# Turning queries and keys on VectorE in 32x32 blocks: a two-layer attention trunk in split fp32

## What is computed

```python
hdn = rms_norm(x, norm_g[i])
q, k, v, z = jnp.split(hdn @ w_in, 4, axis=-1)
q = apply_rope(rms_norm(split_heads(q, N_HEADS), q_norm), cos, sin)   # layer 1: no rope
k = apply_rope(rms_norm(split_heads(k, N_HEADS), k_norm), cos, sin)
s = jnp.einsum('bhqd,bhkd->bhqk', q, k) * d ** -0.5                   # layer 1: + c_q - c_k
y = jnp.einsum('bhqk,bhkd->bhqd', jax.nn.softmax(causal(s)), v)
x = x + (merge_heads(y) * jax.nn.silu(z)) @ w_out[i]
```

## Time and profile before

| | |
|---|---|
| time of three runs, us | 565.17, 565.41, 566.66 |
| the profiled execution's own time, us | 564.39 |
| its span (first to last instruction), us | 562.6 |
| granted TensorE clock over the span | 1.0 |
| busy share: PE, DVE, ACT, POOL | 99%, 60%, 45%, 53% |
| bytes read from HBM, written | 47.48 MB, 2.11 MB |

### The profile page before, as it was taken

One profiled execution on the slowest core, in us unless ns is written; L12 is line 12 of the kernel. 1 busy time (PEld: TensorE's weight loads), 2 busy tenths in 40 slices (PEclk: granted clock), 3 DMA queues, 4 the chain that ended last, 5 costly groups with the idle time before them and its releaser, 6 DMA issues.

```text
span 562.6 us, 9761 instructions
## 1 busy us (share of the span) xinstructions
PE 554.5 (99%) x3086; PEld 512.2 (91%) x3086; DVE 336.4 (60%) x863; ACT 250.4 (45%) x761; POOL 299.5 (53%) x348
## 2 busy tenths in 40 slices
PE   6999999999999999999999999999999999999998
PEld 4999999999999999888898999999999999998887
DVE  3687676767575758472563284746574747564621
ACT  5746262626262626251545454545454545443300
POOL 4766363636362627253655594746574748471700
DMA  9814131313131322122423362615150616040221
GB/s 258 237 38 135 57 93 58 95 56 93 56 93 56 93 56 93 56 77 94 121 58 80 91 138 31 135 35 137 33 152 17 143 28 161 19 149 4 75 94 56
DMA packets 78237, 49.94 MB, mean 89 GB/s; under 512 B 4090, under 2 KB 71418, under 8 KB 78211
## 3 DMA queue, kind: packets, MB, share of 16 engines
q1 hardware_dynamic: 78208, 49.61, 32.8%
q10 hardware_dynamic: 2, 0.00, 0.0%
HBM read 47.48 MB, written 2.11 MB: 88 GB/s over the span
## 4 chain that ended last, share of the span: by engine, by line
PE 96%; DMA 1%; ACT 1%; issue 1%; POOL 1%; DVE 1%; SPq 0%; DVEq 0%; POOLq 0%
PE banks L341 26%; PE banks L342 26%; PE banks L343 26%; PE banks L466 5%; PE banks L451 3%; PE banks L424 2%; PE banks L440 2%; PE banks L439 2%; PE banks L438 2%; PE banks L373 1%; DMA first_raw<-in_a_w_in_dram 1%; ACT probs L648 0%; PE banks L492 0%; PE banks L493 0%; POOL sin_t L1123 0%
## 5 line engine op out<-in xcount | busy, mean ns | idle before, releaser
L1046 POOL TENSOR_TENSOR w_lo<-w_raw,w_hi 128x512 fp32r<-128x512 f32 x147 | 188.1, 1307 | 59.8 <-ACT w_hi L596 59.8
L341 PE MATMUL banks<-w_hi,hT_hi 128*128 128x384 f32 x512 | 175.8, 343 | 2.1 <-DVE hT_lo L785 2.1
L342 PE MATMUL banks<-w_lo,hT_hi 128*128 128x384 f32 x512 | 171.9, 336 | 0.0
L343 PE MATMUL banks<-w_hi,hT_lo 128*128 128x384 f32 x512 | 171.8, 335 | 0.0
L341 PEld LDWEIGHTS banks<-w_hi,hT_hi 128*128 128x128 f32 x512 | 96.6, 189 | 2.7 <-POOL w_lo L1046 2.4
L1062 POOL TENSOR_TENSOR msq<-ssq,eps 128x2 f32<-128x2 f32 x64 | 15.6, 243 | 153.3 <-ACT junk L632 153.2
L342 PEld LDWEIGHTS banks<-w_lo,hT_hi 128*128 128x128 f32 x512 | 96.7, 189 | 0.0
L343 PEld LDWEIGHTS banks<-w_hi,hT_lo 128*128 128x128 f32 x512 | 96.5, 189 | 0.0
L596 ACT ACTIVATE w_hi<-w_raw 128x512 fp32r<-128x512 f32 x148 | 85.0, 643 | 24.5 <-DMA w_raw<-in_b_w_in_dram 19.1
L632 ACT ACTIVATE junk<-banks 128x128 bf16<-128x128 f32 x128 | 34.0, 271 | 110.1 <-PE banks L343 110.0
L908 DVE RECIPROCAL gz<-gz 128x128 f32<-128x128 f32 x64 | 58.2, 933 | 0.5
(11 more groups left out here) (109 smaller groups left out, 891.3 us busy)
## 6 DMA issues: line engine op xcount, KB each, us to landing
w_raw<-in_b_w_in_dram SPq DMA_DIRECT2D x64, 256.0 KB, 4.3
w_raw<-in_a_w_in_dram SPq DMA_DIRECT2D x52, 256.0 KB, 2.9
w_raw<-in_w_out_dram SPq DMA_DIRECT2D x32, 256.0 KB, 3.0
first_raw<-in_a_w_in_dram SPq DMA_DIRECT2D x12, 256.0 KB, 5.6
cos_t<-c_rows SPq DMA_DIRECT2D x8, 256.0 KB, 3.7
out_dram<-xs SPq DMA_DIRECT2D x7, 256.0 KB, 2.1
xs<-in_x_dram SPq DMA_DIRECT2D x3, 512.0 KB, 5.7
xs<-in_x_dram SPq DMA_DIRECT2D x2, 256.0 KB, 2.9
```

The source lines that it names most:

```text
L341: pe.matmul(dst, ah, bh, start=first and m == 0, stop=False)
L342: pe.matmul(dst, ah, bl, start=False, stop=False)
L343: mm = pe.matmul(dst, al, bh, start=False, stop=last and m == n - 1)
L1046: pool.tensor_tensor(w_lo[:, slot, k, :], raw, f32(w_hi[:, slot, k, :]), ALU.subtract).then_inc(wlo_set, by)
```

## The change

TensorE no longer turns queries and keys. VectorE does, in blocks of 32x32: for the two token tiles of one portion, 16 instructions, each of which takes 32 partitions (32 tokens) and, of both q and k and of two tiles, 32 channels, and writes to 32 other partitions of banks 6 and 7. A head has two portions (tiles 0 and 1, tiles 2 and 3), so 32 such instructions. In each engine's period the order is new. The bank of `values` moves from 7 to 3. The plus one of the gate and the division of the probabilities go from DVE to ACT. In `first` the call of TensorE is gone and DVE makes both portions at the end. The core of the diff (the definitions of `silu` and `normalise` move to ACT with the same calls otherwise):

```diff
-        Z_BANK, QT_BANK, Y_BANK = 2, 6, 7
+        Z_BANK, Y_BANK, QT_BANK = 2, 3, 6
 # TensorE
-            def turn_qk(layer, h):
-                pe.wait_ge(qkn_set, TILES * (g + 1))
-                wait(pe, qkTlo_set, 2 * g)
-                wait(pe, y_gated, g)
-                for m in range(2):
-                    for t in range(TILES):
-                        mm = pe.transpose(banks[:, QT_BANK + m, t * P:(t + 1) * P], qkn[:, t, m, :], ident[:, :])
-                    mm.then_inc(qk_turned, 1)
             def scores(layer, h, s):
                 pe.wait_ge(qkTlo_set, 2 * (g + 1))
                 wait(pe, pTlo_set, 3 * g)
+                wait(pe, y_gated, g)
             def period(layer, h, s):
                 qkv(layer, h + 1, 1 - s, 0)
+                qkv(layer, h + 1, 1 - s, 1)
                 scores(layer, h, s)
-                qkv(layer, h + 1, 1 - s, 1)
                 qkv(layer, h + 1, 1 - s, 2)
+                qkv(layer, h + 1, 1 - s, 3)
                 turn_probs(layer, h)
-                qkv(layer, h + 1, 1 - s, 3)
+                zproj(layer, h + 1, 1 - s)
                 values(layer, h, s)
-                zproj(layer, h + 1, 1 - s)
-                turn_qk(layer, h + 1)
             def last(layer):
-                pe.wait_ge(ylo_set, g - 1)
-                pe.wait_ge(vlo_set, TILES * g)
-                project(layer, 0, 0, range(7), True, False)
-                scores(layer, h, 1)
-                project(layer, 0, 1, range(7), True, False)
+                pe.wait_ge(ylo_set, g - 2)
+                pe.wait_ge(qkn_set, TILES * g)
+                project(layer, 0, 0, range(6), True, False)
+                project(layer, 0, 1, range(2), True, False)
+                scores(layer, h, 1)
+                project(layer, 0, 1, range(2, 6), False, False)
+                pe.wait_ge(ylo_set, g - 1)
+                project(layer, 0, 0, [6], False, False)
+                project(layer, 0, 1, [6], False, False)
 # ACT
+            def normalise(layer, h):
+                for n, t in enumerate(T_ORDER):
+                    p = probs[:, P_COL[t]:P_COL[t] + P * (t + 1)]
+                    act.wait_ge(rinv_set, TILES * g + n + 1)
+                    act.activation(p, p, ACT.Copy, scale=rinv[:, t:t + 1]).then_inc(probs_set, 1)
             def exp_z(layer, h):
+                act.wait_ge(ez_set, g + 1)
+                act.activation(gz[:, 0, :], gz[:, 0, :], ACT.Copy, bias=1.0).then_inc(ez1_set, 1)
+            def begin(layer, h):
+                split_qk(layer, h)
+                if not isinstance(h, int) or h > 0:
+                    split_y(layer, h - 1)
             def period(layer, h, s):
+                begin(layer, h)
                 read_qkv(layer, h + 1, 1 - s, 0)
-                split_w(layer, h + 2, s, (0, 1, 2, 3))
+                split_w(layer, h + 2, s, (0, 1, 2))
+                read_qkv(layer, h + 1, 1 - s, 1)
                 exps(layer, h)
-                read_qkv(layer, h + 1, 1 - s, 1)
+                split_w(layer, h + 2, s, (3,))
+                normalise(layer, h)
                 split_w(layer, h + 2, s, (4,))
                 read_qkv(layer, h + 1, 1 - s, 2)
+                split_w(layer, h + 2, s, (5,))
+                read_qkv(layer, h + 1, 1 - s, 3)
                 split_probs(layer, h)
-                split_w(layer, h + 2, s, (5, 6, 7))
-                read_qkv(layer, h + 1, 1 - s, 3)
-                split_y(layer, h)
-                split_qk(layer, h + 1)
+                split_w(layer, h + 2, s, (6, 7))
                 exp_z(layer, h + 1)
 # DVE
+            def turn_qk(layer, h, ts):
+                dve.wait_ge(qkn_set, TILES * g + ts.stop)
+                for a in range(QUADS):
+                    tokens = qkn[a * QUAD:(a + 1) * QUAD, ts, :, :].rearrange("p t m c -> p m t c")
+                    for b in range(QUADS):
+                        turned = banks[b * QUAD:(b + 1) * QUAD, QT_BANK:QT_BANK + 2, ts.start * P:ts.stop * P].rearrange("p m (t c) -> p m t c", c=P)
+                        at = dve.transpose(turned[:, :, :, a * QUAD:(a + 1) * QUAD], tokens[:, :, :, b * QUAD:(b + 1) * QUAD])
+                at.then_inc(qk_turned, 1)
+            def begin(layer, h):
+                late = not isinstance(h, int) or h > 0
+                if late:
+                    gate_y(layer, h - 1)
+                split_qk(layer, h)
+                if late:
+                    low_y(layer, h - 1)
             def period(layer, h, s):
-                silu(layer, h)
+                begin(layer, h)
                 silu_part(layer, h, 0)
+                silu_part(layer, h, 1)
                 split_v(layer, h + 1, 1 - s, 0)
                 norm_qk(layer, h + 1, 0)
+                silu_part(layer, h, 2)
                 maxima(layer, h)
-                silu_part(layer, h, 1)
-                normalise(layer, h)
                 split_v(layer, h + 1, 1 - s, 1)
                 norm_qk(layer, h + 1, 1)
-                silu_part(layer, h, 2)
+                invert_sums(layer, h)
                 silu_part(layer, h, 3)
-                split_probs(layer, h)
+                turn_qk(layer, h + 1, slice(0, 2))
                 split_v(layer, h + 1, 1 - s, 2)
                 norm_qk(layer, h + 1, 2)
                 split_v(layer, h + 1, 1 - s, 3)
-                gate_y(layer, h)
                 norm_qk(layer, h + 1, 3)
-                low_y(layer, h)
-                split_qk(layer, h + 1)
+                split_probs(layer, h)
+                turn_qk(layer, h + 1, slice(2, 4))
 # POOL, period
-                split_w(layer, h + 2, s, (0, 1, 2, 3))
+                split_w(layer, h + 2, s, (0, 1, 2))
                 rstd_qk(layer, h + 1, 1)
-                split_w(layer, h + 2, s, (4,))
+                split_w(layer, h + 2, s, (3, 4))
                 rstd_qk(layer, h + 1, 2)
-                split_w(layer, h + 2, s, (5, 6, 7))
+                split_w(layer, h + 2, s, (5,))
                 rstd_qk(layer, h + 1, 3)
+                split_w(layer, h + 2, s, (6, 7))
```

More of the change, by code:

```diff
@@ L47 @@
 DVE_FIRST = (3, 5, 7)
+QUAD = 32
+QUADS = P // QUAD
 def build_trunk(nc, x, norm_g, w_out, a_w_in, a_q_norm, a_k_norm, b_w_in, b_f_bias, b_q_norm,
@@ L458, in values @@
                 pe.wait_ge(vlo_set, TILES * (g + 1))
-                wait(pe, qkTlo_set, 2 * (g + 1))
                 parts = ((v_hi, pT_hi), (v_hi, pT_lo), (v_lo, pT_hi))
@@ L832, in norm_qk @@
                                   rot[:, t % 2, :, :], ALU.add).then_inc(qkn_set, 1)
+            def turn_qk(layer, h, ts):
+                g = HEADS * layer + h
+                dve.wait_ge(qkn_set, TILES * g + ts.stop)
[5 more added lines that the diff above has]
+                at.then_inc(qk_turned, 1)
             def split_qk(layer, h):
@@ L859, in maxima, with invert_sums @@
                                              accum_out=negmax[:, t:t + 1]).then_inc(max_set, 1)
-            def normalise(layer, h):
+            def invert_sums(layer, h):
                 g = HEADS * layer + h
@@ L894, in low_y @@
                                   ALU.subtract).then_inc(ylo_set, 1)
-            def silu(layer, h):
-                g = HEADS * layer + h
-                dve.wait_ge(ez_set, g + 1)
-                dve.tensor_scalar(gz[:, 0, :], gz[:, 0, :], 1.0, None, ALU.add).then_inc(ez1_set, 1)
             def silu_part(layer, h, n):
@@ L988, in first @@
                     norm_qk(layer, 0, 3)
-                split_qk(layer, 0)
+                for half in range(2):
+                    turn_qk(layer, 0, slice(2 * half, 2 * half + 2))
+            def begin(layer, h):
[5 more added lines that the diff above has]
+                    low_y(layer, h - 1)
             def period(layer, h, s):
-                silu(layer, h)
+                begin(layer, h)
                 silu_part(layer, h, 0)
+                silu_part(layer, h, 1)
                 split_v(layer, h + 1, 1 - s, 0)
                 norm_qk(layer, h + 1, 0)
+                silu_part(layer, h, 2)
                 maxima(layer, h)
-                silu_part(layer, h, 1)
-                normalise(layer, h)
                 split_v(layer, h + 1, 1 - s, 1)
                 norm_qk(layer, h + 1, 1)
-                silu_part(layer, h, 2)
+                invert_sums(layer, h)
                 silu_part(layer, h, 3)
-                split_probs(layer, h)
+                turn_qk(layer, h + 1, slice(0, 2))
                 split_v(layer, h + 1, 1 - s, 2)
@@ L1006, in period @@
                 split_v(layer, h + 1, 1 - s, 3)
-                gate_y(layer, h)
                 norm_qk(layer, h + 1, 3)
-                low_y(layer, h)
-                split_qk(layer, h + 1)
+                split_probs(layer, h)
+                turn_qk(layer, h + 1, slice(2, 4))
             def last(layer):
                 h = HEADS - 1
-                silu(layer, h)
+                begin(layer, h)
+                silu_part(layer, h, 0)
```

(6 more changed lines are left out.)

10 lines of the change are left out of this document (2 added, 8 removed).

## The result

The changed kernel takes 570.39 us (median of five runs, 568.78 to 572.97); the kernel before took 565.17 in five runs beside it. The ratio is 1.0106 (95% interval 1.0087 to 1.0124): slower by 1.1% (by the two medians alone, 0.9%), where 1.1% faster was forecast. The profiled execution is the slowest of the five, 572.97 us with a span of 571.2, so the terms read from it add up to 8.6 us of span and not to the medians' 5.2. Part of that is the clock: TensorE's mean granted clock is 0.988 in this execution and 0.991 in each of the other four.

A forecast was written before the change was run, and what follows sets the result against it. TensorE's list of work was taken to bound the kernel. -14.1 + 6.8 + 0.8 + 1.4 - 0.9 = -6.0 us on the profiled 564.39 gave 558.4, the median 1.0 above: 559.4 us; range 552.0 to 574.0.

The forecast's parts named there:

- What bounds the kernel: Periods of both layers: as long as TensorE's list of work, 27.9 to 28.0 us, so only what leaves it can gain.
- TensorE's gain: Turns of queries and keys leave TensorE: 16 pieces of 0.88 us, 14.1 us in all, periods of 27.05 us.
- The block instruction: VectorE's turn: 0.30 us each, a little over 0.286, run to its end; 32 a head make 9.6 us.
- 0.8 us in all: Layer 0's last six periods and `last`: 0.1 us of waiting in each, as VectorE's list of 26.9 nears TensorE's 27.05.
- the text's own slope: Whole kernel: each 0.01 us of block instruction above 0.30 costs 2.7 us.
- Rival C: Layer 0: VectorE becomes the bound, values wait for `pT_lo` every period; slower above 0.322 us, 574.1 at 0.354; chance 0.28.
- The start of layer 0: First head: TensorE waits 3.7 us for scores, 1.7 for bank 0, 0.2 at tile 3, 1.2 at values; 6.8 together.
- The start of layer 1: First head: TensorE waits 0.8 us for the scores, then 0.6 for bank 0; 1.4 together.
- The walk of the queues: Start of layer 1: queries and keys turned at 320.6, split at 322.6, TensorE there at 321.8.
- What was said to go: Start of layer 1: TensorE's 0.9 us wait for the divisions goes, since probabilities are turned a tile later.
- ACT's and POOL's new work and order: Periods: ACT gains 2.6 us on 13.0, POOL makes its last two `w_lo` later; both counted at nothing.
- the sign: Whole kernel: faster, by 6.0 us; chance 0.64 of faster by over 0.3%, 0.27 of slower.

The follow-up runs named there:

- run 4: Changed kernel with the turn's two loops exchanged, so four block instructions in a row write one partition group and read four; 569.31 us in one run.
- run 5: Changed kernel with each block instruction cut in two, one for queries and one for keys (64 of 32x64 a head); 587.49 us in one run.
- run 12: Changed kernel where, in each layer's first period, ACT reads tile 0 ahead of its copies of the turned queries and keys; 567.59 us in one run.
- run 1: Changed kernel with all turns of queries and keys given back to TensorE, the new order kept; 563.59 us, ratio 0.9986 to the kernel before.
- run 3: Changed kernel with the first head of each layer turned by TensorE, the other seven by VectorE; 557.64 us, ratio 0.9884 to the kernel before.
- run 9: Changed kernel with one 32x256 portion, first heads on TensorE, and the gate's second and third reciprocals behind the inverted sums; 554.80 us, ratio 0.9826.
- run 7: Changed kernel with one 32x256 portion, first heads on TensorE, and the next head's tile 0 normed ahead of the gate's first two reciprocals; 563.35 us, ratio 0.9988.

## Why the prediction was wrong

**What bounds the kernel, and TensorE's gain: right.** The periods of layer 1 went from 27.96 to 27.08 us, 0.88 less. Sixteen times 0.88 is the 14.1 us.

**The block instruction: the term that was mis-sized.** The step reads "I take 0.30 us"; it is 0.335, between the ends that the rows gave. The reason given for it was right, an instruction that changes partition groups is run to its end (runs 4 and 5), but the allowance "a little over" 0.286 was too small: the instruction itself takes 0.322 and the next starts 0.013 later. Why it takes 0.322 and not 0.286, whether for the bank that it writes or for the reordering, no run separates. With it VectorE's list in layer 0 is 17.3 + 10.7 = 28.0 us and the periods are 28.04, about 1 us over TensorE's list in each of seven, where 0.8 us in all was allowed. By the text's own slope, 3.5 hundredths x 2.7 = 9.5 us, the forecast of 559.4 becomes 568.9. That this is near the 570.39 is partly luck: the slope has layer 0 some 3 us too high (8.6 for 6.7 in its periods, 8.5 for 7.2 in its start) and makes up with it for most of what is missing at the start of layer 1. Rival C is what happened, at the place it named (`pT_lo` in each period of layer 0 and nowhere in layer 1) and beyond its turning point of 0.322. The Trainium skill's 311 ns for 128x128 bf16 ("VectorE: DVE Perf Modes", "The three transpose paths") is nearer to the 322 ns of this trace than my choice was, and would still have promised a gain. Its rule on held instructions, in the section "Two Vector instructions with no wait between them" of the same page, agrees with the traces of runs 4 and 5, for the inputs' groups too.

**The start of layer 0: near, and in part by luck.** 6.8 us were forecast at 0.30 us, which at 0.335 would be 8.5. Measured: scores at 52.13, 13.05 us behind the gate projection (8.4 of them two tiles: 4.7 waited), and a first period of 30.6 us, 2.5 over the later ones: 7.2. The split of it was other than told: TensorE ran at the lower clock where it was to wait for bank 0. That cost nothing more, as VectorE has no idle time from 50.8 to 72.2 us and TensorE still waits for it at the values.

**The start of layer 1: the step that failed outright.** It reads "0.8, then 0.6 for bank 0, 1.4 together". Measured: 332.03 - 321.59 - 8.4 = 2.0 us to the scores, and 33.28 - 27.08 = 6.2 in the first period, 8.2 together. Of the first term the block instruction explains what is over 0.8 (32 x 0.035 = 1.1 us); the second, 6.2 for 0.6, was not foreseen. The walk of the queues followed VectorE and TensorE only. ACT's first entry in the period is a wait for the whole turn, and its readings of tiles 0 and 1 stand behind it; POOL's roots, bias and weights stand behind those. Tile 1's norm came 2.6 us late for TensorE, and in the profiled execution the clock fell behind that. Run 12 takes the wait out. In run 4, whose mean clock is that of most executions, this start costs 2.0 us to the scores and 30.45 - 27.08 = 3.4 in the first period, 5.4 together. Of the 3.4 run 12 takes out 1.7, and 1.7 stay with it, where the clock fell behind the first wait.

**What was said to go** (0.9 us of the old wait for the divisions) went, as run 1 shows, but half of it came back at tile 3 of the same period. ACT's and POOL's new work and order cost nothing in the full periods, also as told.

In sum, for the profiled execution: -14.1 as forecast; layer 0's seven longer periods 7 x 0.96 = 6.7 in place of 0.8; its start 7.2 for 6.8; layer 1's start 8.2 for 1.4; -0.9; and 1.3 outside the layers: 8.4 of the 8.6 us of span. The measured time lies inside the range of 552 to 574; the sign was wrong. Neither step alone explains that. With the true block instruction and nothing else amiss, the sum is -14.1 + 6.7 + 7.2 + 2.0 + 0.6 - 0.9 = +1.5 us, an estimate from the terms above and no more than a measurement tells from no change. With the start of layer 1 alone amiss (6.2 for 0.6) it is -0.4. The rest of the loss is the wait and the clock at the start of layer 1, and what differs from one execution to the next.

## What to carry to other kernels

Work given to an idle engine has to be priced at run-to-its-end where neighbours change partition groups, and the receiver's whole list has to be well below the critical engine's: here 0.035 us more on a small instruction, 32 times a head, took back all of a gain of 6 us. Look first at where no earlier work hides the new step: here the two starts cost more than the whole loss, and leaving just the first heads on TensorE turned 1.1% slower into 1.2% faster. And when a wait is placed at the head of an engine's queue, walk every engine that reads from it, since the late one may be two engines on.

## What the runs showed that I had not expected

- Two block instructions that share input and output groups overlap by half of one (0.36 us for two of 0.24), and a new group on either side ends that.
- In the changed kernel TensorE's waits of 4.54 and 2.57 us are followed by a granted clock of 0.55 and 0.50 in the stretches behind them. The wait of 1.93 us is not, but waits of 1.92 and 1.93 us at the same place in runs 4 and 12 are. So these runs give no length of a wait from which the clock falls, and the same program can differ between executions. Without such waits (run 3) the mean over the span is 1.0. What a drop costs depends on what follows it: nothing in layer 0, where VectorE was late anyway, and less at the start of layer 1 in run 4, where the wait behind it was 1.41 us and not 2.57.
- A shorter list did not shorten the round: with 32x256 instructions VectorE has 24.5 us of work in 28.1, and in five runs some 3 us of idle time (2.5 in run 9, 3.7 in run 7) only moved between the four tiles. The last 0.45 us per period between run 9 and TensorE's list is the wait for tile 1's norm; no run here takes it out.
